# Sums, norms and stores of all tiles moved beside the last two experts, whose own tokens are stored over them by index

## The reference

```python
def hier_moe(x, w_rg, b_rg, w_re, b_re, w_eg, w_eu, w_ed):
    ...
    gates = p_g * top_v / jnp.sum(top_v, axis=-1, keepdims=True)
    expert = g[:, None].astype(jnp.int32) * EXPERTS_PER_GROUP + top_i.astype(jnp.int32)
    ...
    def expert_block(args):
        xb, e = args
        h = jax.nn.silu(xb @ w_eg[e]) * (xb @ w_eu[e])
        return h @ w_ed[e]

    ys = lax.map(expert_block, (xs, block_e)).reshape(R, D)
    ys = ys.astype(jnp.float32) * slot_gate[:, None]
    out = jax.ops.segment_sum(ys, slot_tok, num_segments=T + 1)[:T]
    return out.astype(x.dtype)

def encoder_layer(...):
    ...
    h = x + mix.astype(x.dtype)
    hn = rmsnorm(h, norm_ffn).astype(x.dtype).reshape(B * L, D)
    h = h + hier_moe(hn, w_rg, b_rg, w_re, b_re, w_eg, w_eu, w_ed).reshape(B, L, D)
    return h, pool_state, s_new

# in reference():
    y_prompt = rmsnorm(hp[:, N_META:], norm_final).astype(x_prompt.dtype)
    y_sample = rmsnorm(hs, norm_final).astype(x_sample.dtype)
```

## Time and profile before

| | |
|---|---|
| median of 3 runs | 1102.6 us (1100.49 to 1104.8) |
| the profiled execution | 1103.76 us |
| its span, first to last instruction | 1101.9 us |
| granted TensorE clock, mean | 0.966 |
| TensorE busy | 92% of the span |
| VectorE busy | 38% |
| ScalarE busy | 22% |
| GpSimd busy | 10% |
| moved by DMA | 262.17 MB, mean 238 GB/s |

### The profile page before, as it was taken

One profiled execution on the slowest core, in us unless ns is written; L12 is line 12 of the kernel. 1 busy time (PEld: TensorE's weight loads), 2 busy tenths in 40 slices (PEclk: granted clock), 3 DMA queues, 4 the chain that ended last, 5 costly groups with the idle time before them and its releaser, 6 DMA issues.

```text
span 1101.9 us, 32850 instructions
## 1 busy us (share of the span) xinstructions
PE 1012.4 (92%) x14634; PEld 822.7 (75%) x14634; DVE 417.4 (38%) x909; ACT 240.8 (22%) x506; POOL 104.8 (10%) x172
## 2 busy tenths in 40 slices
...
GB/s 272 402 5 39 1 39 0 38 0 38 4 34 38 0 38 1 152 322 173 373 375 393 405 399 411 408 404 401 398 410 403 395 409 404 397 405 401 215 214 300
DMA packets 50850, 262.17 MB, mean 238 GB/s; under 512 B 8205, under 2 KB 10701, under 8 KB 42618
## 3 DMA queue, kind: packets, MB, share of 16 engines
q1 hardware_dynamic: 41050, 234.05, 53.8%
...
...
## 4 chain that ended last, share of the span: by engine, by line
PE 91%; DVE 5%; DMA 2%; issue 1%; ACT 1%; SPq 0%; ACTq 0%; DVEq 0%; POOLq 0%; POOL 0%
PE bank L1412 31%; PE bank L1178 18%; PE bank L1303 11%; PE bank L1423 10%; PE bank L1230 6%; PE bank L1429 5%; PE bank L1166 4%; DVE arena L1144 1%; DVE arena L1142 1%; PE bank L1279 1%; DMA arena<-in_w_in 1%; DVE arena L1150 1%; PE bank L1237 1%; PE bank L1296 1%; PE bank L1290 1%
## 5 line engine op out<-in xcount | busy, mean ns | idle before, releaser
L1178 PE MATMUL bank<-xnT,arena 128*128 128x128 f32 x1728 | 201.5, 278 | 4.9 <-DMA arena<-in_w_in 3.5
L1178 PEld LDWEIGHTS bank<-xnT,arena 128*128 128x128 f32 x1728 | 197.1, 193 | 7.6 <-DMA arena<-in_w_in 4.0
L1412 PEld LDWEIGHTS bank<-xnT,arena 128*64 128x64 f32 x4096 | 171.8, 138 | 8.9 <-issue 8.9
L1412 PE MATMUL bank<-xnT,arena 128*64 128x96 f32 x4096 | 175.0, 248 | 2.2 <-issue 2.2
L1412 PEld LDWEIGHTS bank<-hnT,arena 128*64 128x64 f32 x4096 | 169.6, 137 | 7.4 <-issue 7.4
L1412 PE MATMUL bank<-hnT,arena 128*64 128x96 f32 x4096 | 172.8, 246 | 0.6 <-issue 0.6
L1026 DVE TENSOR_SCALAR mixT<-mixT 128x384 f32<-128x384 f32 x32 | 11.5, 360 | 324.0 <-ACT mixT L692 324.0
L1303 PE MATMUL bank<-arena,mixT 128*128 128x512 f32 x288 | 127.8, 602 | 3.0 <-DVE mixT L859 3.0
L1303 PEld LDWEIGHTS bank<-arena,mixT 128*128 128x128 f32 x288 | 54.9, 193 | 69.4 <-issue 65.7
L1423 PE MATMUL bank<-arena,silu_r 128*32 128x384 f32 x768 | 86.0, 487 | 0.5 <-issue 0.5
L1429 PE MATMUL bank<-arena,silu_r 128*32 128x256 f32 x384 | 85.9, 380 | 0.0
...
## 6 DMA issues: line engine op xcount, KB each, us to landing
...
```

Of the source, the lines that this page charges most:

```text
L1178: last = mm(out, w_in_sb[:, k, a:b], xnT[:, k, :], start=k == 0, stop=k == KD - 1)
L1412: last = mm(out[q * SW:(q + 1) * SW, n * BLOCK:(n + 1) * BLOCK], w[:, k, m * P + q * SW:m * P + (q + 1) * SW], rowsT[b][:, k, :], start=k ...
```

## The change

The tiles are no longer summed after the last expert. When the scatters of experts 0 to 29 have landed, SP loads `pick_rows` into the parts of `arena` that experts 30 and 31 are done with (L460 of the changed kernel; tiles 0 and 1 as expert 30's gate product is done, and so on), and all nine tiles are summed, normalised and stored while experts 30 and 31 run. Rows that belong to tokens of these two experts are then wrong or stale. So that what lies there is at least written, `pick_rows` and a second table `late_rows` are filled with x early in the front. The tokens of experts 30 and 31 are treated by themselves, as rows of those experts (96 at most each): GpSimd gathers their h from a copy of h in DRAM (`h_rows`, stored tile by tile in the front), their gates and expert numbers (`info_rows`), and the output of their other pick; VectorE adds (`late_base`), then adds the expert's own output `ye[b]` from SBUF (`late_sum`), ScalarE takes the norm, VectorE makes the result (`late_out`). When all tile stores have landed, GpSimd writes these rows over `y_prompt` and `y_sample` by index, four indirect DMAs. A token that has both experts 30 and 31 gets expert 30's output through `late_rows`.

Beside that: for tiles 3 to 8 the first half of the sum goes to ScalarE (times the gate, `weight`) and GpSimd (plus h, `pick_half`). The work of VectorE on expert 31 is parted (`gated`, `hidden`) and put between tiles. `g_fin` moves out of `arena` and is loaded before the experts; some buffers of the front are joined to give room. 13 small operations on VectorE go behind the slot table, and the branch for overfull experts gets longer. TensorE's instructions stay as they were, but for waits in that branch.

```diff
+FAR = 8192
+LATE = (NE - 2, NE - 1)
...
+    late_dram = nc.dram_tensor("late_rows", (PICK_ROWS, D), F32, kind="Internal").ap()
+    h_dram = nc.dram_tensor("h_rows", (ROWS, D), F32, kind="Internal").ap()
+    info_dram = nc.dram_tensor("info_rows", (ROWS, 2 * PICKS), F32, kind="Internal").ap()
...
-        y1 = [lot(2 * i) for i in range(TILES)]
-        y2 = [lot(2 * i + 1) for i in range(TILES)]
-        g_fin = lot(2 * TILES)
+        def lot(at):
+            return arena[:, at:at + D]
+        lots = [2 * i * D for i in range(TILES - 1)] + [starts["u", 1]]
+        y1 = [lot(at) for at in lots]
+        y2 = [lot(at + D) for at in lots]
+        g_fin = qk_pooled[:, :]
+        l_h = rows
+        l_sum = [free_work[0:BLOCK, 0:D], k_er[0:BLOCK, :]]
...
+            for k in range(PICKS):
+                sp.dma_start(y_dram[k * ROWS:(k + 1) * ROWS, :], x_all).then_inc(s["filled"], 16)
+                sp.dma_start(late_dram[k * ROWS:(k + 1) * ROWS, :], x_all).then_inc(s["filled"], 16)
...
+            def store_h(j):
+                sp.wait_ge(s["h_added"], j + 1)
+                sp.dma_start(h_dram[j * P:(j + 1) * P, :], h_all[:, j, :]).then_inc(s["h_stored"], 16)
+            for j in range(TILES - 1):
+                store_h(j)
             sp.wait_ge(s["pe_v"], TILES)
             load_weights(0, 0)
             load_weights(0, 1)
+            store_h(TILES - 1)
+            sp.dma_start(g_fin, norm_final.partition_broadcast(P)).then_inc(s["g_fin_in"], 16)
...
+            def load_tile(i):
+                for k, y in ((0, y1[i]), (1, y2[i])):
+                    at_row = k * ROWS + i * P
+                    sp.dma_start(y[0:OUT_ROWS[i], :], y_dram[at_row:at_row + OUT_ROWS[i], :]).then_inc(y_in[i], 16)
+            def store_tile(i):
...
+            sp.wait_ge(s["pe_g"], NE - 1)
+            for b in range(2):
+                sp.wait_ge(ye_stored[b], 16 * (NE // 2 - 1))
+            load_tile(0)
+            load_tile(1)
+            sp.wait_ge(s["pe_u2"], 2 * (NE - 1))
+            load_tile(2)
+            load_tile(3)
+            sp.wait_ge(s["pe_d"], NE - 1)
+            load_tile(4)
+            load_tile(5)
+            sp.wait_ge(s["pe_g"], NE)
+            load_tile(6)
+            load_tile(7)
+            store_tile(0)
+            sp.wait_ge(s["pe_u2"], 2 * NE)
+            load_tile(8)
             sp.wait_ge(s["slots_ready"], 1)
             n_x = sp.value_load(steer[0:1, 0:1], min_val=0, max_val=EXTRA)
-            sp.wait_ge(s["pe_d"], NE)
+            for i in range(1, TILES):
+                store_tile(i)
+            sp.wait_ge(s["outs_stored"], 16 * (2 * PAIRS + 2))
+            sp.wait_ge(s["l_put"], 16 * 2 * NLATE)
...
+            def pick_half(i):
+                pool.wait_ge(s["weighted"], i - 2)
+                nc.gpsimd.tensor_tensor(y1[i], y1[i], h_all[:, i, :], ALU.add).then_inc(s["pool_half"], 1)
+            pool.wait_ge(s["h_stored"], 16 * TILES)
+            pool.wait_ge(s["late_idx_ready"], 1)
+            pool.wait_ge(s["pe_eT"], NE - 1)
+            fetch(l_h[0], h_dram, i_late[:, 0, 0:1], ROWS).then_inc(l_h_in[0], 16)
+            pool.wait_ge(s["info_stored"], 16)
             for b in range(2):
-                scatter(NE // 2 - 1, b)
-
+                fetch(l_info[:, b, :], info_dram, i_late[:, 0, b:b + 1], ROWS).then_inc(s["l_info_in"], 16)
+            for b in range(2):
+                pool.wait_ge(ye_stored[b], 16 * (NE // 2 - 1))
+            for b in range(2):
+                fetch(l_sum[b], y_dram, i_late[:, 1, b:b + 1], PICK_ROWS).then_inc(l_other_in[b], 16)
+            pool.wait_ge(s["pe_eT"], NE)
+            fetch(l_h[1], h_dram, i_late[:, 0, 1:2], ROWS).then_inc(l_h_in[1], 16)
+            pool.wait_ge(s["ye_ready"], YE_STEPS * (NE - 1))
+            put(late_dram, idx_i[:, LATE[0]:LATE[0] + 1], ye[0], PICK_ROWS).then_inc(ye_stored[0], 16)
+            pick_half(3)
+            pool.wait_ge(ye_stored[0], 16 * (NE // 2))
+            pool.wait_ge(l_other_in[1], 16)
+            pool.wait_ge(s["late_idx_ready"], 2)
+            fetch(l_sum[1], late_dram, i_late[:, 4, 1:2], PICK_ROWS).then_inc(s["other_again"], 16)
+            for i in range(4, TILES):
+                pick_half(i)
             pool.wait_ge(s["slots_ready"], 1)
             n_x = pool.value_load(steer[0:1, 0:1], min_val=0, max_val=EXTRA)
-            pool.wait_ge(s["x_idx_ready"], 1)
+            pool.wait_ge(s["tiles_stored"], 16 * TILES)
+            for b in range(2):
+                pool.wait_ge(s["l_out_ready"], b + 1)
+                put(y_prompt, i_late[:, 2, b:b + 1], l_h[b], SEQ).then_inc(s["l_put"], 16)
+                put(y_sample, i_late[:, 3, b:b + 1], l_h[b], SAMPLE).then_inc(s["l_put"], 16)
...
+            def tile_rstd(i):
...
+            def weight(i):
+                act.wait_ge(y_in[i], 16 * PICKS)
+                A(y1[i], y1[i], ACT.Copy, scale=gate_all[:, i, 0:1]).then_inc(s["weighted"], 1)
+            def late_rstd(b):
...
+            act.wait_ge(s["info_ready"], 1)
+            with nc.allow_non_contiguous_dma("four values of each token"):
+                act.dma_start(info_dram.rearrange("(t p) n -> p t n", p=P), info[:, :, :]).then_inc(s["info_stored"], 16)
+            t = NE // 2 - 1
+            gate(t, 0)
+            out_rows(t, 0)
+            tile_rstd(0)
+            gate(t, 1)
+            weight(3)
+            tile_rstd(1)
+            weight(4)
+            tile_rstd(2)
+            weight(5)
+            tile_rstd(3)
+            weight(6)
+            late_rstd(0)
+            weight(7)
+            tile_rstd(4)
+            out_rows(t, 1)
+            weight(8)
+            tile_rstd(5)
+            tile_rstd(6)
+            tile_rstd(7)
+            late_rstd(1)
+            tile_rstd(8)
...
+            def gates_of(st, second, got, g):
...
+            def late_small():
+                dve.wait_ge(s["l_info_in"], 32)
+                st = final.then
+                gates_of(st, k_late[:, :], l_info, l_gates)
...
+                V.tensor_copy(i_late[:, 2:4, :], f_late[:, 2:4, :]).then_inc(s["late_idx_ready"], 1)
+            def first_half(i):
+                dve.wait_ge(y_in[i], 16 * PICKS)
+                r = OUT_ROWS[i]
+                final.then(V.scalar_tensor_tensor(out=y1[i][0:r, :], in0=y1[i][0:r, :], scalar=gate_all[0:r, i, 0:1], in1=h_all[0:r, i, :],
+                                                  op0=ALU.mult, op1=ALU.add))
+            def combine(i):
+                r = OUT_ROWS[i]
+                if i < 3:
+                    first_half(i)
+                else:
+                    dve.wait_ge(s["pool_half"], i - 2)
+                V.scalar_tensor_tensor(out=y1[i][0:r, :], in0=y2[i][0:r, :], scalar=gate_all[0:r, i, 1:2], in1=y1[i][0:r, :],
+                                       op0=ALU.mult, op1=ALU.add).then_inc(s["fin_ready"], 1)
+            def normalize(i):
+                if i == 0:
+                    dve.wait_ge(s["g_fin_in"], 16)
+                dve.wait_ge(s["frstd_ready"], i + 1)
+                r = OUT_ROWS[i]
+                V.scalar_tensor_tensor(out=y2[i][0:r, :], in0=y1[i][0:r, :], scalar=fss[0:r, i:i + 1], in1=g_fin[0:r, :],
+                                       op0=ALU.mult, op1=ALU.mult).then_inc(s["out_ready"], 1)
+            def late_base(b):
+                dve.wait_ge(l_h_in[b], 16)
+                dve.wait_ge(l_other_in[b], 16)
+                if b == 1:
+                    dve.wait_ge(s["other_again"], 16)
+                final.then(V.scalar_tensor_tensor(out=l_sum[b], in0=l_sum[b], scalar=l_gates[:, 1, b:b + 1], in1=l_h[b], op0=ALU.mult, op1=ALU.add))
+            def late_sum(b):
+                dve.wait_ge(s["ye_ready"], YE_STEPS * (LATE[b] + 1))
+                V.scalar_tensor_tensor(out=l_sum[b], in0=ye[b], scalar=l_gates[:, 0, b:b + 1], in1=l_sum[b],
+                                       op0=ALU.mult, op1=ALU.add).then_inc(s["l_sum_ready"], 1)
+            def late_out(b):
+                dve.wait_ge(s["l_rstd_ready"], b + 1)
+                V.scalar_tensor_tensor(out=l_h[b], in0=l_sum[b], scalar=l_ss[:, b:b + 1], in1=g_fin[0:BLOCK, :],
+                                       op0=ALU.mult, op1=ALU.mult).then_inc(s["l_out_ready"], 1)
+            t = NE // 2 - 1
+            expert(t, 0)
+            combine(0)
+            combine(1)
+            late_small()
+            normalize(0)
+            gated(t, 1)
+            combine(2)
+            hidden(t, 1, 0)
+            normalize(1)
+            hidden(t, 1, 1)
+            combine(3)
+            normalize(2)
+            late_base(0)
+            late_sum(0)
+            combine(4)
+            normalize(3)
+            late_out(0)
+            combine(5)
+            normalize(4)
+            combine(6)
+            normalize(5)
+            late_base(1)
+            combine(7)
+            normalize(6)
+            late_sum(1)
+            combine(8)
+            normalize(7)
+            late_out(1)
```

(1 more changed line is left out.)

226 lines of the change are left out of this document (143 added, 83 removed).

## The result

The changed kernel takes 1120.96 us (median of 4 runs, 1120.61 to 1123.92), the kernel before 1103.7 (4 runs, 1100.49 to 1104.84): the ratio is 1.0167, with a 95% interval from 1.0138 to 1.0196. It is 17 us slower, where 1100 was predicted and 1107 was the upper end. Its profiled execution has a span of 1118.8 us against 1101.9, with a granted clock of 0.959.

A forecast was written before the change was run, and what follows sets the result against it. VectorE's list after TensorE was the bound: 34.15 + 4.3 + 3.1 + 9.45 = 51.0 us from 1038.2 to 1089.2, store and puts to 1098.5, plus 1.0: span 1099.5, 1100 us by the median, range 1091 to 1107.

The forecast's parts named there:

- What bounds the kernel before, and where its idle room is: After TensorE's last matmul, VectorE's 27 operations (34.15 us) bind; VectorE idles 10.34 us while the last expert runs.
- rival 2: Late rows' information stored in a full queue comes at 1049, not 1043.2, moving VectorE's list: 5.8 us, 1106; chance 0.13.
- Against it: the queue drains from 1032 on: Argument against the late information store: DMA queues empty from 1032 us, so its small pieces would not wait long.
- The start of the list, 1038.2: VectorE's first tile combination, once tile 0 is loaded behind expert 31's weights; bounds 1036.2 to 1041.2, 26.5 us earlier.
- nothing is queued behind those weights now and the queue drains as they land: Reason for placing tile 0's landing behind expert 31's last weights (1036.4) at 1038.2, nearer the early bound.
- GpSimd's holds: GpSimd's six additions for tiles 3 to 8: five hold VectorE 1.89 us each, 9.45 us; one meets the reciprocal, free.
- rival 1: GpSimd and VectorE don't hold each other on long operations in the tail: 6.8 us less, 1093; chance 0.25.
- TensorE's wait at no price: TensorE's last product starts near 1057 instead of 1047.5 us; its rows, there by 1071, are wanted near 1082.
- Ahead of the tail: Before the late experts: tiny operations and the fill cost nothing; extra queue 1 traffic delays the experts 1.0 us.
- rival 3: The early fill of two tables delays code fetching and stalls the chain: 10 us, 1110; chance 0.10.
- Behind the list: After VectorE's list ends at 1089.2: last store lands 1092.0, four indirect puts end at 1098.2, span 1098.5.
- the 0.3 us that lie behind the last landing before: Span's end after the last DMA landing, taken from the old trace: 0.3 us added behind the fourth put.

## Why the prediction was wrong

**What bounds the kernel before, and where its idle room is:** right. The changed kernel's end is set by VectorE's list, as argued.

**Info late (rival 2):** this is what set the end of the changed kernel: `l_info` was there at 1055.07, where the forecast list, 1.0 us later for the experts, asks for it at 1044.2. Of the 19.3 us, 10.8 are this. The rival's mechanism was right and it deserved far more than 0.13. It was "Against it: the queue drains from 1032 on" that failed: from 1034 to 1056 us the DMA engines were full (1.01 to 1.06), where before their share was 0.25 at 1034 and nothing at 1036. The loads that the change itself brings forward kept them so. The slowest 72 pieces took 27.3 / 72 = 0.38 us each, not 0.23. The price of a packet was right: from 1019.7 to 1047 us queue 1 had 1607 packets in 88.4% of the sixteen engines' time, 0.24 us each. What was wrong is one packet for each piece, it was some 1.6; why, no run shows.

**The start of the list, 1038.2:** wrong by 5.6 us, and outside its own bounds (up to 1041.2). The failing step is "nothing is queued behind those weights now and the queue drains as they land": I priced the loads by the earlier trace rows, on empty queues, and let the weights land when they did before. In the changed kernel they landed at 1042.3 instead of 1036.4. What made them late stays open. Without any tile load behind them they still landed 2 us later than before (19.0 us after the issue), and with them at anything from 18.2 to 30.6; gathers of 393 KB among the loads cost time, as shown, but in the changed kernel three of the four went out after the first combination. Tile 0's half rate was in the 4.81 us that I took for it; what its slow packets cost the transfers beside it was not, and isn't shown apart. Even with nothing ahead of it the first combination came 7.1 us after the issue.

**GpSimd's holds:** right in kind (rival 1 is out: operations of 3.3 us beside the sums), too small by 4.4 us. The sum takes 2.35 us, not the 1.89 that the slope of the earlier trace rows gave for 1024 elements; the estimate by halving the Trainium skill's figure for 2048 elements (GPSIMD Engine Reference, Elementwise), 2.2 us, was the nearer one. All six held something, the tiny operation among them, where I had let one go free beside the reciprocal. That part of the reasoning was sound: with late gathers one sum did meet the reciprocal (2.55 us, as ever) and five operations were held. The sums in turn took up to 3.5 us beside VectorE's operations. That GpSimd's descriptors cost VectorE nothing holds for the indirect DMA at 1047.75 (operations of 1.27 and 1.28 us beside it), but not clearly for the one at 1054.88: the tiny operation of 1055.26 should have been over 0.4 us before the sum began at 1055.84, and ended with it. GpSimd's spans are rough, so this stays open.

**TensorE's wait at no price:** right. It waited until 1072.4, 15 us longer than forecast, and moving it forward by 11 us left the list as long as it was (47.8 against 48.1 us).

**Ahead of the tail:** right. Expert 0's weights were asked for at 459.96 instead of 459.18 us, so the fill delayed no code (rival 3 is out), and the experts began 0.8 us later, where 1.0 was forecast.

**Behind the list:** too small by 6.0 us. The last store landed after 3.4 us, not 2.7, and GpSimd took 0.8 more to issue. The puts stand 1.23 us apart, not 0.95: I took the instruction's 0.94 and left out 0.30 of issue between two. The largest part is the term "the 0.3 us that lie behind the last landing before": 5.2 us lay behind the last put's landing, which itself came 2.1 us after its start and not 3.3. GpSimd's program takes 6.4 us from its last instruction to the end, hidden before, when it ended at 1057, and on the path now.

All in all the list did start 19.9 us earlier than before (1044.83 against 1064.68). But it took 58.7 us where the old one took 34.15, and 15.3 us followed it where 3.1 did: 24.5 + 12.2 - 19.9 = 16.9 us, the difference of the spans (24.53, 12.22 and 19.85 before rounding).
